# First attention of a two-block network on one core: index scores moved between the k-tiles of the projection groups, selection rounds dealt anew

## The reference, cut to what matters

```
q, k, v, qi, ki, wi = jnp.split(h @ w_in, A_SPLITS, axis=-1)
q = rms_norm(q.reshape(B, Tp, N_HEADS, A_HEAD_DIM), gq)
k = rms_norm(k.reshape(B, Tp, A_KV_HEADS, A_HEAD_DIM), gk)
...
    s = jnp.einsum('bqhd,bsd->bqhs', qib, ki) * IDX_DIM ** -0.5
    score = jnp.einsum('bqh,bqhs->bqs', wib, jax.nn.relu(s))
    score = jnp.where(vis[None], score, NEG_INF)
    _, idx = lax.top_k(score, k_top)
```

## Time and profile before

| | us |
|---|---|
| median of 3 runs | 2499.22 |
| lowest and highest run | 2495.83, 2507.11 |
| profiled execution, its own time | 2492.74 |
| its span | 2491.0 |
| TensorE busy | 2389.4 (96%) |
| VectorE busy | 1374.5 (55%) |
| ScalarE busy | 1055.6 (42%) |

### The profile page before, as it was taken

The page is one execution under the profiler, slowest core; times in us unless marked ns, Lnnn a source line. Parts: engine busy times, 40 slices in busy tenths (PEclk is TensorE's granted clock), DMA queues, the critical chain, the costliest instruction groups (busy, mean ns, idle before and its releaser), DMA issues.

```text
span 2491.0 us, 41159 instructions
## 1 busy us (share of the span) xinstructions
PE 2389.4 (96%) x15443; PEld 2133.6 (86%) x15443; DVE 1374.5 (55%) x2103; ACT 1055.6 (42%) x1906; POOL 387.1 (16%) x342
## 2 busy tenths in 40 slices
PE   6999999999999999998989999999999989999999
PEld 5778777887899899887868999999988879999987
DVE  5886677223465245458744666643333455766632
ACT  5645765333343233324444333332455554333322
POOL 0000444700410100100121211100100001211100
PEclk8999999999999999999989999999999989999999
DMA  8563432332333352332102323233422112223233
GB/s 291 163 204 104 114 77 77 101 93 84 93 97 92 99 136 85 101 110 65 44 18 64 93 85 93 86 91 89 135 59 56 50 51 87 83 85 93 84 107 88
DMA packets 413132, 238.42 MB, mean 96 GB/s; under 512 B 11498, under 2 KB 404557, under 8 KB 413029
## 3 DMA queue, kind: packets, MB, share of 16 engines
q1 hardware_dynamic: 404197, 202.25, 28.9%
q0 software_dynamic: 8224, 32.61, 3.8%
q10 hardware_dynamic: 608, 2.16, 0.2%
HBM read 234.54 MB, written 5.00 MB: 96 GB/s over the span
## 4 chain that ended last, share of the span: by engine, by line
PE 82%; DVE 6%; ACT 5%; issue 4%; DMA 3%; POOL 0%; SPq 0%; ACTq 0%; DVEq 0%; POOLq 0%
PE PS L508 61%; PE PS L2076 6%; PE PS L1862 3%; DMA w_raw<-in_w_in_dram 2%; PE PS L2112 1%; PE PS L2207 1%; PE PS L1877 1%; ACT w_hi L429 1%; PE PS L1821 1%; PE PS L1941 1%; DVE w_lo L435 1%; PE PS L2154 1%; PE PS L1977 1%; PE PS L2091 1%; DVE conv_acc L2336 1%
## 5 line engine op out<-in xcount | busy, mean ns | idle before, releaser
L435 DVE TENSOR_TENSOR w_lo<-w_raw,w_hi 128x1024 fp32r<-128x1024 f32 (+2 forms) x376 | 467.5, 1243 | 613.0 <-ACT w_hi L429 611.8
L508 PE MATMUL PS<-op_hi,w_hi 128*128 128x264 f32 (+3 forms) x2440 | 600.2, 310 | 17.0 <-DVE w_lo L435 14.0
L508 PE MATMUL PS<-op_lo,w_hi 128*128 128x264 f32 (+3 forms) x2440 | 597.6, 309 | 0.0
L508 PE MATMUL PS<-op_hi,w_lo 128*128 128x264 f32 (+3 forms) x2440 | 595.2, 308 | 0.0
L429 ACT ACTIVATE w_hi<-w_raw 128x1024 fp32r<-128x1024 f32 (+2 forms) x376 | 378.9, 1008 | 340.4 <-PE PS L508 287.1
L508 PEld LDWEIGHTS PS<-op_hi,w_hi 128*128 128x128 f32 x2440 | 396.8, 189 | 48.4 <-DVE w_lo L435 16.5
L508 PEld LDWEIGHTS PS<-op_hi,w_lo 128*128 128x128 f32 x2440 | 396.2, 189 | 22.5
L508 PEld LDWEIGHTS PS<-op_lo,w_hi 128*128 128x128 f32 x2440 | 395.8, 189 | 21.6 <-issue 0.5
L508 PE MATMUL PS<-ff_hi,w_hi 128*128 128x512 f32 (+1 forms) x784 | 240.4, 343 | 0.0
L508 PE MATMUL PS<-ff_hi,w_lo 128*128 128x512 f32 (+1 forms) x784 | 240.2, 343 | 0.0
L508 PE MATMUL PS<-ff_lo,w_hi 128*128 128x512 f32 (+1 forms) x784 | 239.8, 342 | 0.0
(11 more groups left out here) (497 smaller groups left out, 3808.2 us busy)
## 6 DMA issues: line engine op xcount, KB each, us to landing
w_raw<-in_w_up_dram SPq DMA_DIRECT2D x120, 512.0 KB, 3.8
w_raw<-in_w_in_dram SPq DMA_DIRECT2D x64, 512.0 KB, 4.2
w_raw<-in_w_down_dram SPq DMA_DIRECT2D x64, 512.0 KB, 3.8
w_ada<-in_w_ada_dram POOLq DMA_DIRECT2D x12, 2048.0 KB, 9.2
decay<-sums_scratch SPq DMA_DIRECT2D x16, 512.0 KB, 5.0
w_raw<-in_w_branch_ssd_dram SPq DMA_DIRECT2D x16, 512.0 KB, 3.6
w_raw<-in_w_in_a_dram SPq DMA_DIRECT2D x16, 512.0 KB, 3.8
w_raw<-in_w_kv_b_dram SPq DMA_DIRECT2D x16, 512.0 KB, 4.0
```

Source lines behind the costliest of these rows:

```text
L435: dve.tensor_tensor(wlo[slot][:, 0:ks, :], wraw[slot][:, 0:ks, :], whi[slot][:, 0:ks, :].bitcast(F32), ALU.subtract).then_inc(sem("w_split ...
L508: last = pe.matmul(a[0:l.cols, h, 0:cn], w[slot][:, k, 0:l.cols], x[:, kk, c0:c0 + cn], start=(j == 0 and k == 0 and w is whi and x is l.h ...
```

## The change

The heads of a tile's index scores are no longer one block behind the projection group. index_score(i, h) is one head, and projectA calls it behind k-tile h of the group. Tile s goes in slot s (1 to 4), so between the k-tiles of groups 6 to 9; before, tile s+1 stood in slot s (0 to 3) behind groups 5 to 8. The waits that stood ahead of all scores (rstd, the key product, the copied keys) go to the first two heads. On ScalarE the relus of the tile stand ahead of the evacuation of the group of the slot. On VectorE the sums stand ahead of the weight split, and up to 8 selection rounds of the tile before go between them, one behind each head; ROUNDS is written anew (64 rounds as before).

```diff
-        ROUNDS = {0: (0, 5), 1: (10, 0), 2: (6, 0), 3: (4, 0), 4: (3, 0), 5: (5, 0), 6: (5, 0), 7: (5, 0), 8: (5, 0),
-                  9: (4, 0), 10: (3, 0), 11: (5, 0), 12: (4, 0)}
+        ROUNDS = {1: (0, 6), 2: (8, 1), 3: (6, 0), 4: (5, 0), 5: (6, 0), 6: (5, 0), 7: (5, 0), 8: (6, 0), 9: (4, 0),
+                  10: (4, 0), 11: (4, 0), 12: (4, 0)}
...
+                if 1 <= s <= NT:
+                    index_relu(s)
                 if s < 12:
                     project_outA(5 + s)
...
-                if s < 4:
-                    index_relu(s + 1)
...
-            def projectA(g):
+            def projectA(g, tile=0):
...
-                last.then_inc(sem("units_done"), 1)
+                    if k == KD - 1:
+                        last.then_inc(sem("units_done"), 1)
+                    if tile:
+                        index_score(tile, k)
...
-            def index_scores(i):
+            def index_score(i, h):
                 q0, nq, nk, _ = TT[i]
-                for h in range(QH):
...
+                m = (i - 1) * QH + h
+                e = h % 2
+                if m == 0:
+                    pe.wait_ge(sem("rstd"), RSTD["n3"])
+                    pe.wait_ge(sem("ki_ready"), 1)
+                elif m == 1:
+                    pe.wait_ge(sem("kid_in"), 16)
+                else:
+                    pe.wait_ge(sem("idx_relu"), m - 1)
...
                 if s < 12:
-                    projectA(5 + s)
+                    projectA(5 + s, s if 1 <= s <= NT else 0)
...
-                    pe.wait_ge(sem("rstd"), RSTD["n3"])
-                    pe.wait_ge(sem("ki_ready"), 1)
-                    pe.wait_ge(sem("kid_in"), 16)
-                if s < 4:
-                    index_scores(s + 1)
-                if s == 0:
                     pe.wait_ge(sem("vA"), 1)
...
-            def index_sum(i):
+            def index_sum(i, count):
...
+                    if h < count:
+                        select(1)
...
-                if s:
+                if s > NT:
                     select(ROUNDS.get(s, (0, 0))[0])
                 if s - 1 in NORM_SLOT:
                     head_scaleA(NORM_SLOT[s - 1])
+                if 1 <= s <= NT:
+                    if s == 1:
+                        dve.wait_ge(sem("vA"), 1)
+                    index_sum(s, ROUNDS[s][0])
                 if s < 12:
                     split_nextA(L["ia"], 5 + s)
-                if s < 4:
-                    if s == 0:
-                        dve.wait_ge(sem("vA"), 1)
-                    index_sum(s + 1)
+                if 1 <= s <= NT:
                     select(ROUNDS[s][1])
```

More of the change, by code:

```diff
@@ L1906, in turn_valuesA @@
                 pe.transpose(PS[0:META, 7, 0:P], rs[:, 4 * P:T], ident).then_inc(sem("vA_trans"), 1)
-            def index_scores(i):
+            def index_score(i, h):
                 q0, nq, nk, _ = TT[i]
-                for h in range(QH):
[L1911 to L1923, removed]
+                m = (i - 1) * QH + h
[7 more added lines that the diff above has]
+                    pe.wait_ge(sem("idx_relu"), m - 1)
+                rows = slice(64 * e, 64 * e + 64)
+                q, k = iq[rows, h // 2, q0:q0 + nq], (kid if e else kwt)[rows, :]
+                if nk <= 512:
+                    last = pe.matmul(PS[:, 4 + 2 * e, 0:nk], q, k[:, 0:nk], start=True, stop=True)
+                else:
+                    for a in range(2):
+                        last = pe.matmul(PS[:, 4 + 2 * e + a, 0:nk // 2], q, k[:, a * nk // 2:(a + 1) * nk // 2],
+                                         start=True, stop=True)
+                last.then_inc(sem("idx_ps"), 1)
             def logitsA(n):
```

## The result

The changed kernel takes 2529.82 us (median of 4 runs, 2527.0 to 2531.99), the one before 2498.07 in the same comparison: 1.0133 times as long, 95% interval 1.0115 to 1.015. Forecast was no change (2501, range 2491 to 2510). The forecast was wrong. What happened has the trigger of rival B (the new gaps) and the state of rival C (whole groups at 1.2 GHz), at some two thirds of C's price.

A forecast was written before the change was run, and what follows sets the result against it. TensorE was taken as the bound, with 82% of the chain of waits. Terms 2.3 + 23.6 + 26.8 + 2.8 (head squares) + 6.9 = 62.4 us against 60.71, +1.7, gave 2501 us, range 2491 to 2510.

The forecast's parts named there:

- rival B: TensorE's clock falls at the new gaps, each fall costing 1.4 to 2.6 us; +5.7 us, 2505; chance 20%.
- rival C: Alternating projection and score counts as light work, clock stays 1.2 GHz through groups 6 to 9; +43, 2542 us; chance 4%.
- Start (2.3 us): From the turned weights to group 6, which waits for ScalarE's copy of them: 2.3 us.
- Four groups at full clock (23.6): Projection groups 6 to 9 on TensorE at full clock, 4 x 5.9 = 23.6 us.
- Scores (26.8): Index scores between k-tiles on TensorE: columns 17.9 us plus fixed cost 8.9 us, sum 26.8.
- the fixed part: Cost of a lone head beside its columns on TensorE: 0.29 us, 8.9 us in all.
- Bounds of 0.11 and 0.55: Fixed cost per head: 0.11 us with switches free (scores 21.4), 0.55 with open weight loads and both switches (35.5).
- Rival A: Switches of tiling mode on TensorE are cheap and hidden, 0.11 us per head; -3.7 us, 2495.5; chance 15%.
- The estimate of 21 us for the scores: Scores priced from the skill's pipe drain of about 128 cycles: 0.053 us per switch, 0.11 per head.
- Boundaries (6.9): TensorE waits for ScalarE's evacuation at group boundaries, gaps of 1.55, 1.7, 1.8 and 1.85: 6.9 us.
- VectorE and ScalarE at nothing: Relus, sums, weight splits and moved selection rounds were costed at nothing, with no slack on VectorE at two points.
- Rival D: VectorE runs late, holding relus and then scores in groups 7 and 8, 2 us once; +4, 2503; chance 6%.

The follow-up runs named there:

- e2_fill: Changed kernel plus twelve unread matmuls of 264 columns on all rows ahead of groups 7, 8 and 9; 2507.8 us, 1.0033 of before.
- e7: Changed kernel with groups 6 to 9 taking two PSUM bank pairs in turn and turned weights in bank 7; 2497.08 us, 0.9995 of before.
- e4_pairs: Changed kernel with an even and an odd head's scores issued together behind every second k-tile; 2492.24 us, 0.9971 of before.
- e8: e7 with the waits for the previous group's evacuation put back ahead of groups 7, 8 and 9; 2524.3 us, 1.0109 of before.
- e3_rounds: Kernel before with the changed kernel's selection rounds per slot, scores left as blocks behind the groups; 2500.18 us, 1.0012 of before.
- e1: Changed kernel with groups 6 to 9 taking two pairs of PSUM banks in turn, without waiting for evacuation; 2502.69 us, 1.0019 of before.

## Why the prediction was wrong, by its own steps

**Start (2.3 us).** Right: 2.30.

**Four groups at full clock (23.6).** This is the step that failed. It took the end of slow clock in groups 6 and 7 as a gain and put the chance that the new stream holds the clock down at 4%. Two of four groups ran at half clock, behind the new gaps. Its price by spacing: tile 2 went by 2.82 us per k-tile and head against 1.58 at full clock (e2_fill), tile 4 by 3.67 against 2.01 (e7): 8 x (1.24 + 1.66) = 23.2, plus 1.7 at the squares (1150.94 to 1155.42, 4.48 us for 2.82), 24.9 of the 29.7 us.

**Scores (26.8).** The mechanism was right, the fixed part mis-sized. At full clock the four spacings are 1.37, 1.58, 1.80 and 2.01; less 0.733 for six projection matmuls and the columns (0.24, 0.45, 0.67, 0.88) it is 0.40 each time, not 0.29. The missing 0.11 is the first projection matmul behind a score: in the rows above 1124.09 to 1124.44 is 0.35 for a pair that else takes 0.245. It could have been read in the trace of before: the pair at 1160.53 was followed after 0.35 too, by this row:

```profile
1160.88 0.40 PE L1862 MATMUL PS<-op_lo,w_hi 128*128 128x264 f32 x2
```

32 x 0.11 = 3.5 us. Bounds of 0.11 and 0.55 held it. Losing the side-by-side heads was the second cause, and it was named; e4_pairs gives it back. Rival A, cheap switches, is refuted by the 0.40. The estimate of 21 us for the scores left out the 0.11 of the first pass that the same rows show; with it, it would have been 24.9.

**Boundaries (6.9).** Size right: the profile's 1.39, 1.49, 1.60 and 1.71 count from the modelled end of the last matmul; in starts, 1125.03 to 1126.92 is 1.89, less 0.34 of the two passes is 1.55 as forecast. What they do was wrong. "Nothing fills it" was priced as idle time alone. e8 against e7 prices two of these gaps at 27 us, of which the gaps themselves are 3.0; the rest is the slow clock behind them.

**VectorE and ScalarE at nothing.** Right. No score waited for a relu in the changed kernel, and e3_rounds shows the deal of rounds free. Rival D fell.

**Sum.** At full clock, as an estimate: 90.43 - 24.9 = 65.5 against 62.4 forecast; the difference is about the 3.5 of the fixed part. That would have been about 5 us over before, inside the range. So without the slow clock the forecast of no change would have stood, with part of the error hidden in the width of its range.

**Rivals B and C.** B gave 1.4 to 2.6 us per fall, read from before, where a dense group followed each fall: 48 matmuls with no score between, full clock again after 3 to 6 us (0.67 over 8.53 us, 0.81 over 7.30). That price can't be carried to a stream with scores in it: there a fall can end as soon (e2, group 6), but it lasted 17 us in e1, and it cost 9.9 us in tile 2 and 13.3 in tile 4. B had the trigger, and was put at 20%; its mechanism was the right one, and what failed in it was the length of a fall. C had the state (clock 0.5 through a group) and the point of decision (11 us lost), but took the stream alone as its cause: e7 has the stream and 1.00. The evidence I held against C, scores of tiles 3 and 4 alone at 1.00 with a quarter idle, came from blocks of 7 to 8 us between dense groups, and said nothing of 12 to 30 us in a row. What in the stream holds the clock down, the half of the rows, the switches or something else, no run separates. The Trainium skill, TensorE: Matmul & The Clock Gate, "A second HAM failure mode", has small idle pieces between groups as the cause of a clock that goes up and down; the trace agrees on the cause (clock 0.5 behind gaps of 1.39 and 1.60 us) and shows more: it stayed down for at least 24 and 31 us.

## What to carry to other kernels

Price a gap of TensorE by what follows it. Ahead of dense matmuls a fall of the clock costs a few us; ahead of a long stretch in which matmuls on half of the rows stand one by one between the dense ones it can cost nearly as much as the stretch itself: 13.3 us on the 16.1 of eight k-tiles with the scores of tile 4. It does not do so each time, so one profile without a fall proves little. Work that uses half the rows is best issued in pairs that run side by side, also when it is spread between other matmuls, and a second pair of PSUM banks takes the gap away.

## What was not expected of the hardware

A wait of 1.4 to 1.6 us, with TensorE otherwise never idle, was followed by 24 and 31 us at 1.2 GHz, although TensorE was busy for 94% of those windows. A float32 head on 64 rows that stands alone between matmuls on 128 rows costs 0.40 us beside its columns at full clock, with 144 columns as with 528: 0.09 going in, 0.11 between its two passes, 0.09 going out and 0.11 in the first matmul afterwards. Two heads on different halves of the rows, queued together, take 0.87 us where one takes 0.86.
